# A transformer block in float32 on one core: the first feed-forward product by Strassen's seven half-size products

## The reference

```python
mix = jnp.concatenate([y_da, y_mla], axis=-1) @ w_o[l]
h = h + _rms(mix, g_attn_post[l])
u = _rms(h, g_mlp_pre[l])                      # the norm's weights g_mlp_pre multiply each feature
f = jnp.square(jax.nn.relu(u @ w_ff1[l])) @ w_ff2[l]
h = h + _rms(f, g_mlp_post[l])
return h[:, N_META:]
```

## Time and profile before

| | us |
|---|---|
| median of 3 runs | 2994.44 |
| runs, lowest and highest | 2991.07, 2994.64 |
| the profiled execution | 2988.28 |
| its span, first to last instruction | 2986.3 |
| feed-forward stage on PE within it | 1551.1 to 2971.0 |

### The profile page before, as it was taken

One profiled execution on the slowest core, in us unless ns is written; L12 is line 12 of the kernel. 1 busy time (PEld: TensorE's weight loads), 2 busy tenths in 40 slices (PEclk: granted clock), 3 DMA queues, 4 the chain that ended last, 5 costly groups with the idle time before them and its releaser, 6 DMA issues. The chain is left out here.

```text
span 2986.3 us, 36186 instructions
## 1 busy us (share of the span) xinstructions
PE 2805.1 (94%) x12988; PEld 2287.8 (77%) x12988; DVE 1405.2 (47%) x2811; ACT 1000.1 (33%) x1628; POOL 495.8 (17%) x322
## 2 busy tenths in 40 slices
PE   6999897699996999979979999999999999999997
PEld 5996686466674888867758888888887888888886
DVE  5113303688893766644424334344345343443444
ACT  6112212477673555545532111121113111211112
POOL 0010001122220222210012121121114111211112
PEclk8999998799998999989989999999999999999999
DMA  5323316833415011033551111111145111111113
GB/s 185 120 105 93 99 46 224 217 83 81 114 40 159 26 43 36 26 99 113 169 169 57 57 42 46 52 42 56 42 148 176 43 44 55 42 55 43 42 49 99
DMA packets 221510, 256.72 MB, mean 86 GB/s; under 512 B 18496, under 2 KB 169520, under 8 KB 219472
## 3 DMA queue, kind: packets, MB, share of 16 engines
q1 hardware_dynamic: 221392, 255.22, 28.3%
HBM read 182.59 MB, written 72.59 MB: 85 GB/s over the span
## 5 line engine op out<-in xcount | busy, mean ns | idle before, releaser
L2357 DVE TENSOR_TENSOR ff_acc<-ff_acc,ff_ps 128x1024 f32<-128x1024 f32 x240 | 292.3, 1218 | 719.3 <-PE ff_ps L2431 719.3
L2414 PE MATMUL ff_ps<-ff_u_hi,ff_w_hi 128*128 128x512 f32 x1024 | 406.4, 397 | 12.5 <-DVE ff_w_lo L2345 12.5
L2414 PE MATMUL ff_ps<-ff_u_lo,ff_w_hi 128*128 128x512 f32 x1024 | 406.0, 396 | 0.0
L2414 PE MATMUL ff_ps<-ff_u_hi,ff_w_lo 128*128 128x512 f32 x1024 | 405.9, 396 | 0.0
L2431 PE MATMUL ff_ps<-ff_w_hi,ff_hid_hi 128*128 128x512 f32 x1024 | 399.3, 390 | 1.3 <-DVE ff_acc L2357 1.2
L2431 PE MATMUL ff_ps<-ff_w_lo,ff_hid_hi 128*128 128x512 f32 x1024 | 399.1, 390 | 0.0
L2431 PE MATMUL ff_ps<-ff_w_hi,ff_hid_lo 128*128 128x512 f32 x1024 | 398.4, 389 | 0.0
L2322 ACT ACTIVATE work<-ff_ps 128x1024 f32<-128x1024 f32 x64 | 65.6, 1025 | 739.8 <-PE ff_ps L2414 739.8
L2286 POOL TENSOR_TENSOR work<-work 128x1024 f32<-128x1024 f32 x64 | 121.2, 1894 | 1081.7 <-ACT work L2322 1081.7
L1410 PE MATMUL da_ps_s<-da_keys,da_qs 128*128 128x420 f32 (+17 forms) x704 | 222.4, 426 | 34.7 <-DMA late_ident<-in_ident 16.3
L2414 PEld LDWEIGHTS ff_ps<-ff_u_hi,ff_w_hi 128*128 128x128 f32 x1024 | 193.0, 188 | 59.3 <-DVE ff_w_lo L2345 12.9
(11 more groups left out here) (200 smaller groups left out, 4996.4 us busy)
## 6 DMA issues: line engine op xcount, KB each, us to landing
ff_w_raw<-in_w_ff SPq DMA_DIRECT2D x64, 512.0 KB, 4.2
work<-in_w_ff SPq DMA_DIRECT2D x64, 512.0 KB, 3.4
ni_xt<-in_x SPq DMA_DIRECT2D x16, 512.0 KB, 4.0
mo_y<-scr_yT SPq DMA_DIRECT2D x16, 512.0 KB, 6.0
work<-in_x SPq DMA_DIRECT2D x16, 512.0 KB, 5.0
scr_h<-mo_h SPq DMA_DIRECT2D x16, 512.0 KB, 3.4
ff_h_in<-scr_h SPq DMA_DIRECT2D x16, 512.0 KB, 4.3
out<-ff_acc SPq DMA_DIRECT2D x16, 512.0 KB, 5.2
```

What stands on the lines that cost most here:

```text
L2357: dve.tensor_tensor(acc[:, t], acc[:, t], ps2[t % 2][:, :], ALU.add).then_inc(part_added, 1)
L2414: m = pe.matmul(ps1[e][:, cols], w[:, e, k], a[:, k, cols], start=k == 0 and i == 0, stop=k == KD - 1 and i == 2)
```

## The change

`mlp` now takes four groups of 512 tokens and, in each, 16 pairs n of 128-feature blocks (64 pairs in all). Each pair's product of 256 features by 512 tokens over 1024 is cut in 2x2 blocks (feature halves, token halves of 256, input halves of 512) and done by Strassen's scheme: seven products instead of eight, each of sums or differences of blocks. They run in the order 3, 5, 1, 2, 4, 6, 7; products 6 and 7 are accumulated onto products 3 and 5 in PSUM.

- `w_sums` on POOL: five sums of blocks of `w_ff1` of 512 elements a partition for each pair. `u_sum` on POOL: five sums of blocks of the tokens of 1024 elements, once in a group.
- Seven high and seven low parts of 512 elements for each pair (`s_high`, `s_low`), seven of 1024 of the tokens for each group (`b_high`, `b_low`).
- `hidden` on PE: 7 products x 4 k x 3 = 84 matmuls of 256 columns. `parts`: 4 tiles x 12 matmuls of 512 columns of the pair before, as one piece behind `hidden`.
- ACT copies products 5, 2 and 4 out of PSUM (`copy_m`, 256 elements), and DVE puts the four quarters together in `pre` by five operations (`upper_right`, `left_and_rest`, `lower_right`, `upper_left`), before relu and squares.
- The weights are loaded four times instead of twice: `w_ff1` 1 MB for each pair, issued when all seven low parts of the pair ahead are made; `w_ff2` 1 MB for each pair.
- The norm's weights are multiplied into the tokens in `mix_out` (DVE, one operation with `g_pre` out of `ps_t`, in place of ACT's copy and DVE's subtraction); `gain` is gone. `mix_out` keeps 512 tokens in SBUF, unsplit, and stores the rest unsplit.

```diff
-                def gain(n):
-                    pool.tensor_tensor(w1_raw[:, :, :], w1_raw[:, :, :], g_pre[:, :].unsqueeze(2).broadcast_to([P, KD, P]),
-                                       ALU.mult).then_inc(w1_gained, 1)
...
+                        dve.tensor_tensor(u_place(s, u, stays), ps_t[:, :].rearrange("p (k t) -> p k t", k=KD),
+                                          g_pre[:, :].unsqueeze(2).broadcast_to([P, KD, P]), ALU.mult).then_inc(u_ready, 1)
...
+    ORDER = (3, 5, 1, 2, 4, 6, 7)
...
+                def w_sums(n):
+                    if not static(n, 0):
+                        pool.wait_ge(w1_loaded, 16 * n)
+                    for j, i in enumerate(W_SUM_ORDER):
+                        a, b, c, d, op = W_SUMS[i]
+                        pool.tensor_tensor(s_sum[:, j], w_block(a, b), w_block(c, d), op).then_inc(s_sum_ready, 1)
...
+                def body(n, u, G, c):                                  # POOL
+                    if not static(n, NPAIR - 1):
+                        w_sums(n + 1)
+                    if c == NC - 1 and G < NGR - 1:
+                        for i in U_SUM_ORDER[:2]:
+                            u_sum(G + 1, i)
+                    squares(n)
...
+                    if c == 0 and G:
+                        for t in range(TG):
+                            add_h(pool, TG * (G - 1) + t)
...
+                hold(sp, s_lo_ready, 7)
+                load_w1(1, 2 * P)
...
+                    if not (isinstance(n, int) and n + 2 >= NPAIR):
+                        hold(sp, s_lo_ready, 7 * n + 14)
+                        load_w1(n + 2, column(n, G, 2))
...
+                    for i in (3, 5, 1, 2, 4):                          # ACT
+                        if i in (5, 4):
+                            copy_m(n, *((5,) if i == 5 else (2, 4)))
+                        if more:
+                            s_high(n + 1, i)
+                        if turn and i in (3, 5):
+                            b_high(G + 1, i)
...
+                    if not begins:                                     # DVE
+                        w2_low(n - 1)
+                    upper_right(n)
+                    weights(3, 5)
+                    tokens(3)
+                    left_and_rest(n)
+                    weights(1)
+                    tokens(5)
+                    lower_right(n)
+                    weights(2)
+                    upper_left(n)
+                    weights(4)
+                    hid_low(n, u, 0)
+                    tokens(1)
+                    added(0)
+                    weights(6)
+                    hid_low(n, u, 1)
+                    weights(7)
+                    tokens(2)
+                    added(1)
...
+                        if i in (6, 7):                                # PE
+                            pe.wait_ge(pre_step, POSTS * n + 1)
+                        for k in range(HK):
+                            for j, (w, a) in enumerate(((s_hi, b_hi), (s_hi, b_lo), (s_lo, b_hi))):
+                                m = pe.matmul(place[i], w[:, at, k], a[:, at, k], start=i not in (6, 7) and k == 0 and j == 0,
+                                              stop=k == HK - 1 and j == 2, skip_group_check=i in (6, 7))
```

More of the change, by code:

```diff
@@ new lines, in squares @@
+                def squares(n):
+                    for j, b in enumerate((1, 0)):
+                        if not static(n, 0):
+                            pool.wait_ge(hid_lo_ready, 2 * n - 1 + j)
+                        pool.wait_ge(relu_ready, 2 * n + j + 1)
+                        pool.tensor_tensor(square[:, b], pre[:, b], pre[:, b], ALU.mult).then_inc(square_ready, 1)
+                pool.memset(eps[:, :], EPS).then_inc(eps_set, 1)
+                u_sum(0, U_SUM_ORDER[0])
+                w_sums(0)
@@ new lines, in body @@
+                def body(n, u, G, c):
+                    turn, more = c == NC - 1 and G < NGR - 1, not static(n, NPAIR - 1)
+                    if not static(n, 0):
+                        w2_high(n - 1)
+                    for i in (3, 5, 1, 2, 4):
[5 more added lines that the diff above has]
+                            b_high(G + 1, i)
+                    for j in range(2):
+                        hidden(n, u, j)
+                        if turn and j == 0:
+                            b_high(G + 1, 1)
+                    for i in (6, 7):
+                        if more:
+                            s_high(n + 1, i)
+                        if turn:
+                            b_high(G + 1, {6: 2, 7: 4}[i])
+                    if turn:
+                        b_high(G + 1, 6)
+                        b_high(G + 1, 7)
+                    if c == 0 and G:
+                        for t in range(TG):
+                            norm(G - 1, t)
@@ new lines, in scale, with body, weights, tokens @@
+                def scale(G, t):
+                    n = TG * G + t
+                    dve.wait_ge(stat_step, 3 * n + 3)
+                    dve.scalar_tensor_tensor(out=acc[:, t], in0=acc[:, t], scalar=stat[:, 2:3], in1=g_post,
+                                             op0=ALU.mult, op1=ALU.mult).then_inc(post_ready, 1)
+                for i in ORDER:
+                    s_low(0, i)
+                    b_low(0, i)
+                dve.wait_ge(post_gain_loaded, 16)
+                def body(n, u, G, c):
+                    turn, more = c == NC - 1 and G < NGR - 1, not static(n, NPAIR - 1)
+                    ends, begins = c == 0 and G, c == 0 and not G
+                    def weights(*which):
+                        for i in which:
+                            if more:
+                                s_low(n + 1, i)
+                    def tokens(*which):
+                        for i in which:
+                            if turn:
+                                b_low(G + 1, i)
+                    def added(t):
+                        if not begins:
+                            add(n - 1, t, G, first=u == 1 and static(c, 1))
+                    if not begins:
+                        w2_low(n - 1)
[17 more added lines that the diff above has]
+                    added(1)
+                    if ends:
+                        scale(G - 1, 0)
+                    tokens(4)
+                    added(2)
+                    if ends:
+                        scale(G - 1, 1)
+                    tokens(6, 7)
+                    added(3)
+                    if ends:
+                        scale(G - 1, 2)
+                        scale(G - 1, 3)
@@ L2453, with body @@
+                def body(n, u, G, c):
+                    hidden(n, G, c)
+                    if not static(n, 0):
+                        parts(n - 1, 1 - u)
+                walk(pe, body)
+                parts(NPAIR - 1, 1)
 class Arrays:
```

494 lines of the change are left out of this document (261 added, 233 removed).

## The result

The changed kernel took **3109.5 us** (median of 4 runs, 3108.1 to 3112.6) where the kernel before took 2993.2 (4 runs, 2991.1 to 2994.6): a ratio of 1.0391 with a 95% interval of 1.0373 to 1.0409. Slower, by 116 us; the forecast was 3133, its range 2960 to 3250. The profiled execution took 3109.2 us, its span 3107.4.

A forecast was written before the change was run, and what follows sets the result against it. A resource shared by POOL and DVE was to make PE wait: 1544.6 to the stage, 75 start, 62 pairs of 22.7 (1407.4), 77 turns, 14.6 last parts, 12.8 end and 2.0 around the span, 3133 us; range 2960 to 3250.

The forecast's parts named there:

- steady pair T: Feed-forward loop: time between successive pairs, 22.7 us, taken as half each of 23.2 and 22.2.
- first matmul of pair 2: Start of the feed-forward stage: pairs 0, 1 and the parts of 0 end at 1544.6 + 75 = 1619.6 us.
- a turn: Change between token groups: three pairs of about 37, 25 and 32 us, 26 us extra each turn, 77 in all.
- exclusive resource: Feed-forward pair: DVE's low parts and all POOL operations exclude each other, using 16.1 us of a 20.7 us pair.
- hand timeline: One steady pair scheduled by hand, POOL and DVE alternating on the shared resource: 23.2 or 22.2 us by order.
- the longer case: Steady pair where POOL's second square goes ahead of DVE's first hidden low part: 23.2 us.
- the load loop closes at 23 on its own account: Loading w_ff1: 17.4 us from landing to the last low part plus 5.8 us for the next load.
- The sign that I had named for that loop: PE idle before product 3, released by `ff_s_lo`, with pairs 22 to 23.3 us apart.
- A: Rival: waits fall into DVE's free time, pair 20.7 us, 2958 us (2936 or 2990 with other turns); chance 0.20.
- 256-column matmul: Product on PE: matmuls start 0.117 us apart, 84 take 9.8 us where there were 11.2.
- start's saving of 2.9 us: Mixing stage loses an ACT copy and a store, so the stage's first instruction moves from 1547.5 to about 1544.6.
- Rival C: POOL keeps the resource through its queued sums, delaying `upper_right`: pair 24.5 us, whole 3245 us; chance 0.12.

The follow-up runs named there:

- e2: Changed kernel with each of POOL's weight sums replaced by two fills that read nothing: 3012.4 us.
- e1: Changed kernel without POOL's five weight sums for each pair, all seven products taking blocks of w_ff1 itself: 3004.0 us.
- e4: Changed kernel with DVE's additions of tiles 0 and 1 each moved ahead of the low parts that stood before them: 3033.2 us.
- e3: Changed kernel with the next w_ff1 asked for once nothing reads the loaded one, and POOL's sums waiting for the previous pair's low parts: 3017.4 us.
- e7: Changed kernel with early load, additions first and reordered last pairs, plus two residual additions behind the weight sums in a group's second pair: 3005.2 us.
- e5: Changed kernel with ACT's copy of product 5 ahead of the high part of token block 3 in a group's last pair: 3111.1 us.
- e11: Changed kernel with early load, additions first, first sums in the mixing stage, four token sums ahead of turns, reordered turns: 2983.8 us, ratio 0.9977.

## Why the prediction was right, point by point

| term | predicted | measured |
|---|---|---|
| PE alone, a pair | 20.7 | 20.98 |
| steady pair T | 22.7 (22.2 or 23.2) | 22.27 |
| stage's first instruction | 1544.6 | 1547.2 |
| first matmul of pair 2 | 1619.6 | 1620.4 |
| a turn | 26 | 26.3 |
| last pair to the end | 50.1 | 50.9 |
| execution | 3133 | 3109.2 |

- **The exclusive resource** holds: 1.806 us for a sum, 0.995 and 1.427 for low parts that take 0.693 and 1.075 when POOL's sums only write (e2), and 1.214 for what reads PSUM. Without POOL's reads of the weights the pair is PE's 20.98 (e1, e2).
- **The 24 us too much** are almost all T: 62 x 0.43 = 27. The hand timeline had `added(0)` end at 17.5 (POOL first) or 16.5 (DVE first); it ended at 16.4. Its two low parts of `w_ff2` were given 3.55 us and took 3.45; POOL's five sums ended at 10.6 and not at 11.4, so all behind them was 0.8 to 1.1 early. The order at the second square was POOL first, as in the longer case. That case was priced at 23.2 and came at 22.27; halving the difference to the other case brought the forecast to 22.7, and that much of its nearness is luck.
- **A step that failed:** "because the load loop closes at 23 on its own account". The load took 5.5 us as estimated, but e4 ran at T 21.01 with the load asked for after the seventh low part as before. I had taken the loop's 17.4 us from landing to the last low part as fixed, and its stretches are not: they were 16.5 here and 15.4 in e4. The sign that I had named for that loop, PE idle before product 3 and released by `ff_s_lo`, does not appear: in the steady stretch PE waits for `ff_acc` alone. What fits all of it is one loop, through DVE's chain, PE's tiles 2 and 3 and the load; an edit that frees either link tried (e3, e4) takes it to PE's bound. So A, a pair at PE's bound, was nearer than its chance of 0.20 said: two additions, each moved ahead of one low part, reach it.
- **The 256-column matmul** takes 0.120, not 0.117: 0.25 us a pair. The product gained 11.2 - 10.08 = 1.1 us a pair and not 1.4, 72 us in 64.
- **The start's saving of 2.9 us** is not to be seen: the table load came at 1547.24 here against 1547.48, and the same stage began anywhere between 1542.5 and 1549.0 in e1 to e7. The sum came right because the prologue took 73.1 instead of 75 from there: two errors that cancel, by luck. (By their own terms A's two other values are 2937 and 2991, not 2936 and 2990; nothing rests on them.)
- **The turn** was right in size (26 and 26.3; its three pairs forecast at 37, 25 and 32 took 38.2, 22.6 and 32.3) and in its first wait (product 6 from 7.2 to 13.9 us into the pair; forecast 7.0 to 14.3), though not in what that wait was worth: taking it away gave nothing (e5), since the queue behind it was late for the same reason.
- **Rival C** fell: POOL does not keep the resource through its queue. In the pair shown, DVE's low parts come in between the sums one by one (1799.77, 1803.72).

What the loss is made of, by the table (121 us between the two stages, 116 between the medians): the product saves 72 us; the turns cost 79, the start 33 more than the 40 us that before needed for that share (3.7 + 36.4), and the stretched chain 61 x 1.29 = 79. With T at 20.98 (e3) the stage is 1473; with start and turns cut to 51.1 and 17.8 (e11) it is 1435.9, 3 us under before. The product's 72 us are still nearly all spent, on 53 us of turns and on a start of 51.1.

## What to carry to other kernels

Count the operations of POOL and DVE that read two operands in SBUF as one engine, and put DVE's PSUM reads beside POOL's work. Where PE misses its bound by a microsecond in each round of a loop, look for the link that is cheapest to free (an addition ahead of a low part, a load asked for when its last reader is done) before the algorithm is judged; here that was worth 72 us (e4) and 87 us (e3) of a stage that had grown by 121. A wait taken out of a turn says nothing until the sum over all pairs of the turn is smaller. And an algorithm that saves a tenth of one product has to pay for every restart that its smaller groups bring.
